# Differential attention on one core: bias, scale and row minimum in one VectorE operation on negated logits, and one factor for the second map

## What is computed

```python
def block(args):
    qblk, bi = args
    q_pos = bi * Q_BLOCK + jnp.arange(Q_BLOCK)
    rel = q_pos[:, None] - k_pos[None, :]
    mask = rel >= 0
    bias = jnp.moveaxis(rel_bias[t5_bucket(rel)], -1, 0).astype(jnp.float32)

    def probs(qi, ki):
        logits = jnp.einsum('bhqd,bhkd->bhqk', qi, ki).astype(jnp.float32) * scale + bias
        return jax.nn.softmax(jnp.where(mask, logits, -jnp.inf), axis=-1)

    a = probs(qblk[..., 0, :], k1) - lam * probs(qblk[..., 1, :], k2)
    return jnp.einsum('bhqk,bhkv->bhqv', a.astype(v.dtype), v)
...
o = diff_attention(dq, dk, dv, rel_bias, lam)
o = rms_norm(o.transpose(0, 2, 1, 3), subln_w) * (1.0 - lam_init)
```

## Time and profile before

| | us |
|---|---|
| median of 3 runs | 3279.6 |
| lowest and highest | 3277.45, 3280.17 |
| span of the profiled execution, first to last instruction | 3282.4 |
| PE busy | 3081.2 (94%) |
| DVE busy | 1652.2 (50%) |
| ACT busy | 1052.2 (32%) |
| POOL busy | 217.4 (7%) |
| mean granted TensorE clock | 0.965 of full |

### The profile page before, as it was taken

How to read it: one execution, slowest core, us unless ns; L and a number is a source line. 1 busy time by engine, 2 the same in 40 slices (tenths; PEclk the granted TensorE clock), 3 DMA queues, 4 the chain that set the end, 5 groups by cost and what they waited for, 6 DMA issues and landing times.

```text
span 3282.4 us, 42167 instructions
## 1 busy us (share of the span) xinstructions
PE 3081.2 (94%) x17336; PEld 2348.3 (72%) x17336; DVE 1652.2 (50%) x3143; ACT 1052.2 (32%) x2148; POOL 217.4 (7%) x165
## 2 busy tenths in 40 slices
PE   8999999989999999999999889999899999898887
PEld 6777778767888878888778778888687888333333
DVE  5444485375655555555584565444654674221212
ACT  4222244353323243333344343222333453000002
POOL 0000012221000000000022230000000110000000
PEclk9999999989999999999999889999899889899999
DMA  5543421112223222122211012232212005999997
GB/s 184 183 168 141 150 97 52 39 39 97 96 77 119 87 97 84 65 84 71 90 65 45 33 52 90 89 109 84 80 65 78 2 2 207 367 421 421 421 421 328
DMA packets 66168, 443.39 MB, mean 135 GB/s; under 512 B 7476, under 2 KB 7732, under 8 KB 19640
## 3 DMA queue, kind: packets, MB, share of 16 engines
q1 hardware_dynamic: 61632, 425.75, 34.0%
q10 hardware_dynamic: 2648, 8.39, 0.7%
q0 software_dynamic: 1696, 6.55, 0.5%
HBM read 435.16 MB, written 5.51 MB: 134 GB/s over the span
## 4 chain that ended last, share of the span: by engine, by line
PE 73%; DVE 11%; DMA 6%; ACT 4%; SPq 3%; issue 1%; POOL 0%; ACTq 0%; DVEq 0%
PE ps L180 72%; DVE b L200 5%; DMA b<-in_eg 5%; SPq L154 3%; DVE b L190 3%; ACT b L206 2%; DVE b L195 1%; ACT b L205 1%; PE ps L309 1%; ACT b L411 1%; DVE b L2079 1%; DVE b L196 0%; DMA h_scratch<-b 0%; POOL b L190 0%; DMA b<-in_xt 0%
## 5 line engine op out<-in xcount | busy, mean ns | idle before, releaser
L180 PE MATMUL ps<-b,b 128*128 128x512 f32 (+6 forms) x14038 | 2793.3, 391 | 138.8 <-DVE b L190 49.5
L180 PEld LDWEIGHTS ps<-b,b 128*128 128x128 f32 (+3 forms) x14038 | 2090.3, 183 | 806.3 <-issue 307.0
L190 DVE TENSOR_TENSOR b<-b,b 128x1024 fp32r<-128x1024 f32 (+7 forms) x743 | 610.8, 827 | 282.7 <-ACT b L411 164.6
L411 ACT CAST b<-b 128x1024 fp32r<-128x1024 f32 (+2 forms) x408 | 391.7, 962 | 406.0 <-PE ps L180 398.5
L190 DVE TENSOR_TENSOR b<-ps,b 128x64 f32<-128x64 f32 (+5 forms) x626 | 220.0, 366 | 299.9 <-PE ps L180 246.9
L180 PE MATMUL ps<-b 64*64 64x64 f32 (+10 forms) x2848 | 249.2, 277 | 31.2 <-ACT b L2045 17.4
L190 POOL TENSOR_TENSOR b<-b,b 128x1024 fp32r<-128x1024 f32 (+3 forms) x112 | 183.1, 1653 | 1368.6 <-ACT b L411 939.7
L180 PEld LDWEIGHTS ps<-b 64*64 64x64 f32 (+3 forms) x2848 | 212.2, 160 | 63.8 <-ACT b L2045 19.7
L200 DVE SCALAR_TENSOR_TENSOR b<-ps,b 128x512 f32<-128x512 f32 (+3 forms) x272 | 142.5, 546 | 209.9 <-PE ps L180 183.4
L206 ACT ACTIVATE b<-b 128x512 f32<-128x512 f32 (+7 forms) x287 | 151.3, 533 | 212.1 <-DVE b L200 171.1
L190 DVE TENSOR_TENSOR b<-b,ps 128x512 f32<-128x512 f32 (+1 forms) x114 | 77.1, 678 | 278.6 <-PE ps L180 275.9
(11 more groups left out here) (106 smaller groups left out, 569.0 us busy)
## 6 DMA issues: line engine op xcount, KB each, us to landing
b<-in_eg SPq DMA_DIRECT2D x64, 1024.0 KB, 26.4
b<-in_eu SPq DMA_DIRECT2D x64, 1024.0 KB, 27.0
b<-in_ed SPq DMA_DIRECT2D x64, 1024.0 KB, 27.0
b<-in_wg SPq DMA_DIRECT2D x44, 1024.0 KB, 4.8
b<-in_wu SPq DMA_DIRECT2D x44, 1024.0 KB, 4.9
b<-in_win SPq DMA_DIRECT2D x40, 1024.0 KB, 4.8
b<-in_wd SPq DMA_DIRECT2D x48, 768.0 KB, 4.2
b<-in_wmod SPq DMA_DIRECT2D x24, 1024.0 KB, 4.9
```

The costliest lines, as they stand in the source:

```text
L180: return e.h.matmul(out, l, r, start=start, stop=stop)
L190: return e.h.tensor_tensor(out, a, b, op)
L411: e.h.copy(hi, src).then_inc(*self.S.tick(("hi", i)))
```

## The change

The table bias4 is kept times sqrt(32), so that (product + bias4) times -1/sqrt(32) is the negated logit. One fused operation per map, tensor_tensor_reduce, writes that and its row minimum, which is the negated row maximum. The exponential is taken with scale -1 and that minimum as its bias, and waits for its own map only. The combined map is made without the first sum's inverse: map2 times (sum1 · lam / sum2), minus map1. This is the combination times -sum1; 1/sum1 is applied when ScalarE reads the product with the values, and the sign is in the norm's weights, sl_0 and sl_1.

```diff
@@ Modulation.dve, step "rel"
-                tt(e, self.F[:, h, c0:c0 + n], k.bank[4 + h][:, 0:n], self.neg[:, c0:c0 + n], ALU.add).then_inc(
-                    *self.V.tick(("F", i, h)))
+                stt(e, self.F[:, h, c0:c0 + n], k.bank[4 + h][:, 0:n], 32.0 ** 0.5, self.neg[:, c0:c0 + n], ALU.mult,
+                    ALU.add).then_inc(*self.V.tick(("F", i, h)))
@@ Modulation.dve, step "MOD"
-                for n, s in ((f"mn_{l}", 0.5), (f"sl_{l}", 0.2 + 0.6 * math.exp(-0.3 * l))):
+                for n, s in ((f"mn_{l}", 0.5), (f"sl_{l}", -0.2 - 0.6 * math.exp(-0.3 * l))):
@@ Mixer.diff_act
-            e.h.copy(self.Yd[:, t, h * 64:h * 64 + 64], B[7][:, 0:64]).then_inc(*S.tick(("yd", u)))
+            act(e, self.Yd[:, t, h * 64:h * 64 + 64], B[7][:, 0:64], ACT.Copy, scale=self.mx[u % 3][:, 6:7]).then_inc(
+                *S.tick(("yd", u)))
...
-            e.wait_ge(V.at(("neg", n)))
             for c in range(2):
                 L = self.Lg[n % 3][c]
-                act(e, L[:, 0:w], L[:, 0:w], ACT.Exp, m[:, 2 + c:3 + c], acc=m[:, 4 + c:5 + c]).then_inc(*S.tick(("ex", n, c)))
+                e.wait_ge(V.at(("L", n, c)))
+                act(e, L[:, 0:w], L[:, 0:w], ACT.Exp, m[:, 2 + c:3 + c], -1.0, acc=m[:, 4 + c:5 + c]).then_inc(*S.tick(("ex", n, c)))
@@ Mixer.diff_dve
-            tt(e, m[:, 8:9], m[:, 7:8], self.lam[:, 5:6], ALU.mult).then_inc(*V.tick(("lamr", u)))
+            stt(e, m[:, 8:9], m[:, 4:5], m[:, 7:8], self.lam[:, 5:6], ALU.mult, ALU.mult).then_inc(*V.tick(("lamr", u)))
             e.wait_ge(V.at(("lamr", u)))
-            ts(e, L[1][:, 0:w], L[1][:, 0:w], m[:, 8:9], ALU.mult).then_inc(*V.tick(("second", u)))
-            e.wait_ge(V.at(("second", u)))
-            stt(e, L[0][:, 0:w], L[0][:, 0:w], m[:, 6:7], L[1][:, 0:w], ALU.mult, ALU.subtract).then_inc(*V.tick(("Aw", u)))
+            stt(e, L[0][:, 0:w], L[1][:, 0:w], m[:, 8:9], L[0][:, 0:w], ALU.mult, ALU.subtract).then_inc(*V.tick(("Aw", u)))
...
-                stt(e, self.Lg[x][c][:, 0:w], B[2 + c][:, 0:w], 32.0 ** -0.5, self.k.bias4[:, h, 512 - w:512], ALU.mult,
-                    ALU.add).then_inc(*V.tick(("L", n, c)))
-            for c in range(2):
-                e.wait_ge(V.at(("L", n, c)))
-                e.h.reduce_max(m[:, c:c + 1], self.Lg[x][c][:, 0:w], AX).then_inc(*V.tick(("max", n, c)))
-            e.wait_ge(V.at(("max", n, 1)))
-            ts(e, m[:, 2:4], m[:, 0:2], -1.0, ALU.mult).then_inc(*V.tick(("neg", n)))
+                e.h.tensor_tensor_reduce(self.Lg[x][c][:, 0:w], B[2 + c][:, 0:w], self.k.bias4[:, h, 512 - w:512], -32.0 ** -0.5,
+                                         3.0e38, ALU.add, ALU.min, m[:, 2 + c:3 + c]).then_inc(*V.tick(("L", n, c)))
```

## The result

| | before | changed |
|---|---|---|
| median of 4 runs, us | 3279.89 | 3257.17 |
| lowest, highest | 3277.45, 3287.95 | 3253.44, 3262.92 |
| span of the profiled execution | 3282.4 | 3251.6 |
| first differential logits to first output product, mixer 1 | 88.88 | 75.17 |
| the same, mixer 2 | 90.12 | 78.44 |

The ratio is 0.9928, with a 95% interval from 0.9909 to 0.9947: 23 us or 0.7% faster; 3254 was forecast, with a range of 3240 to 3272. The last two rows, which I call the stage, are read from TensorE's timeline; they sum to 25.4 us won (26 were forecast). The profiled execution gains 30.8 us, 5.4 more than the stages; it is at the lower edge of its runs, and in it TensorE's clock is at its lower level for 196 us in all against 233 before, some of that far from the change.

The account below looks back on a forecast made before the run. A latency loop through VectorE and ScalarE was taken to bound the differential attention stage. Gaps and clock (6.3, 2.7, 2.0, 1.3, 0.7) gave 13.0 us per mixer, 26 for both: about 3254 us, range 3240 to 3272.

Parts of the forecast that it names:

- The bound: Differential attention: from 641.6 to 687.7 us the chain of waits runs only through VectorE and ScalarE, never touching TensorE.
- The price of the fused operation: Per map at 512 keys: 0.68 us plus a read, 0.78 in all; 0.36 us more per tile.
- The turn: One tile's loop through VectorE and ScalarE: 2.2 of 5.7 us saved at 512 keys, 0.9 of 3.4 at 128.
- The gaps: TensorE's waits per mixer, 18.6 us: first five shrink from 9.2 to 2.9, the two at 701.78 and 705.25 lose 2.0.
- The tail: Gaps at 719.76, 723.58 and 728.63, where gates and norms come before the wait: 0.7 us won.
- POOL: Its gating products hold VectorE's factor and combination, two SBUF inputs each; only the removed product's loss is taken back.
- The clock: TensorE's low clock behind gaps: 2.7 us back of 4.5, plus 1.3 us at 689.75 and 707.36, per mixer.
- ScalarE's read: ScalarE's 16 reads of the product, now with a scale per row: same 0.20 us each, no cost.
- B: TensorE's and ScalarE's order takes over early: gaps give 8 us per mixer, clock nothing; 3264 us, chance 0.18.
- C: Fused operation costs as much as the two it replaces, 1.36 us at 512: gain about 12 us, 3268; chance 0.12.
- D: Slower kernel: fused operation at three times today's duration plus the read, 2.15 us; loses 11 us, 3291; chance 0.05.
- E: No change: what is won goes into the tail of VectorE's gates and norms and POOL's products; chance 0.03.

Follow-up runs that it names:

- rival C's run: Changed kernel plus an unused row maximum over the bias table behind each fused operation, with the tick behind that: 3266.4 us, ratio 0.9947.
- both moves: Changed kernel with gating products on VectorE instead of POOL, and the second output weight block's split behind step diff 17: 3234.3 us, ratio 0.9856.

## Why the prediction was right

**The bound.** Right. The chain without TensorE for 46 us was the signal, and 72% of the stages' gain stay when more than half of VectorE's work is put back (rival C's run). What the share of busy time could not say, the order of waits did.

**The price of the fused operation.** I took 0.68 us plus a read that pushes the second map to 0.78. It is 0.69, and the second map starts after 0.62. The term of 0.36 us per tile for the reads should have been near 0. ScalarE's read, from which I took it, holds its successor back by 0.1 us; VectorE's doesn't. I also wrote that no row had a scalar-tensor-tensor operation with two fp32 inputs in SBUF; the combination is one, 0.75 us at 512, and could have tested the Trainium skill's sentence ahead of any run.

**The turn.** At 512 keys I gave 3.60 us from logits to next logits; in the timeline it is 3.48 (650.25 to 653.73); at 128, the old 3.0 less the forecast 0.9 is 2.1, against 1.96 (640.79 to 642.75). The reads cost less, and ScalarE's second exponential doesn't start when its map is ready but when the first exponential has ended, which takes most of that back.

**The gaps.** I worked out one mixer and doubled it, as the gaps were the same "to 0.1 us". One is not: the gap of 1.92 us at 687.72 is 2.97 us in the second mixer, so the second had 19.7 us of gaps and not 18.6. In order of time, forecast and measured in the first mixer: 0.85 and 0.66, 0.7 and 0.50, 0.3 and 0.35, 0.4 and 1.07, 0.65 and 0.68. The fourth is the one I mis-sized ("almost gone"): I had the logits "free 5 us earlier" and forgot at that place what I had written under POOL, that factor and combination are both held (2.52 us from 660.87). The next two, 2.4 left of 4.4, are 1.93. The tail, 4.3 left of 5.0, is 3.5 in the first mixer and 4.9 in the second. In all 10 us of gaps per mixer went (9.9 and 9.6), 9.0 were forecast.

**The clock.** I counted on 4.0 us back per mixer, most of it (60% and a half) of what I took low clock to cost. The stage without its gaps shrank by 3.8 us in the first mixer and by 2.1 in the second, where more gaps closed than forecast (9.9 and 9.6 against 9.0). So 13.7 and 11.7 meet the 13.0 in the mean with too little clock and a little more gap, and partly by luck. Place by place it was less right: the ten half blocks of 24 products lost 5.6 us in the first mixer and lose 3.6 now, 4.8 and 4.0 in the second. Of the 1.3 us expected back at 689.75 and 707.36, 0.1 came (4.49 and 4.25 became 4.60 and 4.00), and the half block at 674.74, meant to take 3.1 to 4 us, takes 4.22 and 5.08. I had also taken the low clock's cost too low, 7.1 us per mixer: with both moves in addition the same work takes 9.5 us less than before in the first mixer.

**ScalarE's read** is not of equal price as I wrote, 0.31 us against 0.20, but it costs nothing on TensorE's path (run with the plain copy). The modulation's scaled sums I did not test.

**The rivals.** B (ScalarE's order takes over) is half right in its mechanism: of the remaining gaps of the first mixer five of nine are released by ScalarE's copy, but with 2.8 of 8.7 us, so they are small. C is out by the row of 0.69. Its consequence was wrong too: at its price 17 us of gain are left by the ratio, 18.2 in the stages, where C said 12. D needed an operation of 1.9 us. E's tail did stay (2.83 became 2.78), and the gain passed by it: what ran in front of it came earlier too.

## What to carry to other kernels

Read the chain of waits for stretches in which the busiest engine doesn't appear: there the order of small operations on two other engines sets the time, and each that goes or starts earlier shortens the stage until the bound comes back, though not by its full length: the scaled second map, 6.8 us of VectorE's work per mixer, was worth 3.1 and 2.2 us alone. After such a change read again what the remaining gaps wait for: a held operation that had been one link of a long loop may now stand alone in TensorE's way. Moving two such pieces of work was worth as much again as the change, and 3 us without it; the gaps it closed were as long in both cases, and the clock made the difference. Look behind the end of a stage too, as a gap closed in it can open just behind. Where POOL held VectorE, a 128x1 operation took 1.03 us in place of 0.16, so place the other engine's long instructions where VectorE reads PSUM or has nothing to do.

## What was not expected of the hardware

- The fused operation's accumulator read (0.08 us) costs no time: the next operation starts with it, 0.62 us behind the first at 512 elements.
- A fused operation with both inputs in SBUF takes 0.69 us at 512 fp32 elements, as with one in PSUM; beside POOL it took 2.09.
- A VectorE operation of two numbers per row took 1.25 us instead of 0.17, and four of 256 elements took 4.42 instead of 1.43 us, while POOL subtracted 1024 columns (and, in the second case, made its squares behind that).
- What a closed gap brings back in clock differs widely: the two moves closed 8.3 us of gaps behind the change and made the stages 20.1 us shorter (granted clock 0.91 and 0.87, then 0.97 and 0.95); in the kernel before they closed 8.0 us and made them 6.4 us shorter (0.85 throughout).
